# One inference step of a hybrid decoder layer: the transition from attention to experts reordered, and a front that accumulates the query projections over half of the features while the other half of the modulation arrives

## What is computed

```python
h = rmsnorm(x, ln_mix_g) * (1.0 + sc1) + sh1
z = h @ w_in                       # 19 column blocks of 512: queries are the first two
x = x + g1 * ((ga * oa + gb * ob + gc * oc) @ w_out)
h2 = rmsnorm(x, ln_ffn_g) * (1.0 + sc2) + sh2
logits = h2 @ router_w + router_b  # top 4 of 32 experts per token
...                                # per expert: w1 (1024 x 2048), gated, w2 (1024 x 1024)
x = x + g2 * f
```

## Time and profile before

| what | value |
|---|---|
| median of 3 runs | 1566.5 us (1562.74 to 1569.09) |
| the profiled execution's own time | 1566.85 us |
| its span in the trace | 1564.5 us |
| PE busy | 1479.6 us, 95% |
| mean granted PE clock | 0.973 of full speed |
| HBM read | 490.14 MB |

### The profile page before, as it was taken

The page is one execution under the profiler, slowest core; times in us unless marked ns, Lnnn a source line. Parts: engine busy times, 40 slices in busy tenths (PEclk is TensorE's granted clock), DMA queues, the critical chain, the costliest instruction groups (busy, mean ns, idle before and its releaser), DMA issues.

```text
span 1564.5 us, 21084 instructions
## 1 busy us (share of the span) xinstructions
PE 1479.6 (95%) x8234; PEld 628.3 (40%) x8235; DVE 648.6 (41%) x1001; ACT 338.3 (22%) x610; POOL 128.7 (8%) x118
## 2 busy tenths in 40 slices
PE   4989899999999978999999999999999999999997
PEld 3455455554555452333333333333333333333332
DVE  2141223445246472444353443443444435344444
ACT  2123332212223132212112121121121211212121
POOL 0000000213227703000000000000000000000000
PEclk8989999999999987999999999999999999999998
DMA  9663542342233975999999999999994999999994
GB/s 350 225 248 117 232 164 98 119 125 108 89 114 118 286 309 220 428 426 427 428 429 429 429 429 429 428 429 429 377 428 170 429 429 429 428 428 428 428 429 201
DMA packets 40269, 495.22 MB, mean 317 GB/s; under 512 B 5316, under 2 KB 5860, under 8 KB 11428
## 3 DMA queue, kind: packets, MB, share of 16 engines
q1 hardware_dynamic: 35700, 480.18, 74.2%
q0 software_dynamic: 4528, 14.46, 3.4%
HBM read 490.14 MB, written 4.47 MB: 316 GB/s over the span
## 4 chain that ended last, share of the span: by engine, by line
PE 81%; DMA 12%; DVE 3%; ACT 1%; POOL 1%; issue 1%; SPq 0%; POOLq 0%; DVEq 0%
PE ps L1866 25%; PE ps L1459 18%; PE ps L1891 14%; DMA memory<-in_w_moe 9%; PE ps L1470 4%; PE ps L1816 4%; PE ps L1801 4%; PE ps L1412 3%; DMA memory<-in_w_dense 1%; DMA memory<-mod_rows 1%; PE ps L1428 1%; PE ps L1873 1%; PE ps L1524 1%; DMA consts<-in_consts 1%; PE ps L1551 1%
## 5 line engine op out<-in xcount | busy, mean ns | idle before, releaser
L1866 PE MATMUL ps<-memory,arena 128*64 128x512 f32 x2176 | 483.9, 596 | 9.8 <-DMA memory<-in_w_moe 9.8
L1459 PE MATMUL ps<-memory,xT 128*128 128x512 f32 x672 | 308.5, 616 | 6.4 <-DMA memory<-in_w_dense 6.4
L1866 PEld LDWEIGHTS ps<-memory,arena 128*64 128x64 f32 x2176 | 152.3, 137 | 301.8 <-issue 277.0
L1891 PE MATMUL ps<-memory,arena 128*64 128x512 f32 x1088 | 248.4, 598 | 0.1
L1459 PEld LDWEIGHTS ps<-memory,xT 128*128 128x128 f32 x672 | 129.4, 197 | 163.4 <-issue 155.3
L1891 PEld LDWEIGHTS ps<-memory,arena 128*64 128x64 f32 x1088 | 72.3, 136 | 145.9 <-issue 134.7
L1388 DVE TENSOR_TENSOR R<-R,xT 128x1024 f32<-128x1024 f32 (+1 forms) x102 | 124.7, 1222 | 3.5
L1377 DVE TENSOR_SCALAR arena<-ps 128x512 f32<-128x512 f32 x34 | 23.5, 692 | 230.8 <-PE ps L1873 230.8
L1385 DVE SCALAR_TENSOR_TENSOR xT<-ps,arena,mod 128x1024 f32<-128x1024 f32 x68 | 87.1, 1281 | 10.1 <-PE ps L1816 10.1
L1816 PE MATMUL ps<-xT,arena 64*128 64x512 bf16 x630 | 87.6, 386 | 2.9 <-DVE xT L1394 2.9
L856 ACT ACTIVATE xT<-ps 128x512 f32<-128x512 f32 x35 | 20.9, 599 | 310.2 <-PE ps L1801 301.4
(11 more groups left out here) (299 smaller groups left out, 1189.6 us busy)
## 6 DMA issues: line engine op xcount, KB each, us to landing
memory<-in_w_moe SPq DMA_DIRECT2D x192, 2048.0 KB, 22.7
memory<-in_w_dense SPq DMA_DIRECT2D x33, 2048.0 KB, 8.6
memory<-in_state POOLq DMA_DIRECT2D x8, 256.0 KB, 7.3
out_sample_retention<-memory POOLq DMA_DIRECT2D x8, 256.0 KB, 5.2
memory<-mod_rows SPq DMA_DIRECT2D x4, 512.0 KB
arena<-in_b POOLq DMA_DIRECT2D x9, 128.0 KB, 2.6
R<-in_x_prompt SPq DMA_DIRECT2D x1, 1024.0 KB, 10.4
arena<-in_cache_kT POOLq DMA_DIRECT2D x8, 128.0 KB, 3.5
```

What stands on the lines that cost most here:

```text
L1459: last = mm(banks[t][0], xT[:, k, t * P:t * P + P], wv[:, k, :], start=(k == 0), stop=(k == KD - 1))
L1866: last = mm(ps[64 * a:64 * a + 64, half, :], xgT[:, k, j % 2, :], wv[:, k, HALF * a:HALF * a + HALF], start=(j % 2 == 0 and k == 0), stop= ...
L1891: last = mm(ps[64 * a:64 * a + 64, 2, :], actT[:, k, j - 4, :], wv[:, k, HALF * a:HALF * a + HALF], start=False, stop=(j == 5 and k == 3), ...
```

## The change

Three things change together.

**The front.** The order of the dense units becomes `ada` 2, 0, 3, 1, AKV, ...; AQ0 and AQ1 leave the ring and go to slots 3 and 4, and SP issues them right behind `ada` 0, without a wait. With scale and shift of features 0 to 511 there, PE accumulates k = 0 to 3 of four query pieces (AQ0 and AQ1, tiles 0 and 1) and of AQ0's tile 2, with `modulation(3)` and `modulation(1)` in between, and adds k = 4 to 7 later. The high four groups are copied out of PSUM unscaled first (`xT_raw`), since their banks are the ones that the pieces need, and scaled in place afterwards. The small matrix `ident` is the second transfer instead of the sixth. POOL's first loads wait for `ada1` instead of `ada0`.

**The transition's transfers.** The prompt's gain rows go to another place (`V[:, 1, :]`) and are loaded before the sample's first gate; expert unit 3 is issued behind the shift rows instead of ahead of them; DVE waits for the prompt's gain alone before the first residual.

**The transition's order.** On DVE `normalise(0)` stands behind `mean_square(1)`, `choose_experts(0)` and `(1)` follow one another, and `normalise(2)` stands behind `choose_experts(2)`. PE counts experts tile by tile with wider products, gathers the first block before the table's product, and POOL's `memset` of `y_parts` waits for `first_picked`.

```diff
-DENSE_ORDER = [("ada", 2), ("ada", 3), ("ada", 0), ("ada", 1), ("proj", AQ0), ("proj", AQ1), ("proj", AKV),
+DENSE_ORDER = [("ada", 2), ("ada", 0), ("ada", 3), ("ada", 1), ("proj", AKV),
...
+RING_UNITS = len(DENSE_ORDER)
+DENSE_ORDER += [("proj", AQ0), ("proj", AQ1)]
...
         sp.dma_start(silu_c, ins["c"]).then_inc(c_in, 16)
+        sp.dma_start(ident, ins["consts"][:, 0:P]).then_inc(select_in, 16)
         load_unit(0)
...
         load_unit(1)
+        load_unit(proj_unit(AQ0))
+        load_unit(proj_unit(AQ1))
         load_unit(2)
...
         load_rows(V[:, 0, :], 4, gate1_in)
+        load_rows(V[:, 1, :], 8, gain2_in)
         load_rows(V[0:64, 2, :], 4, gate1_in)
...
         sp.wait_ge(merged, 3)
-        load_rows(U[:, 2, :], 8, gain2_in)
-        load_rows(U[0:64, 1, :], 8, gain2_in)
-        load_expert_unit(3)
+        load_rows(U[0:64, 1, :], 8, gain2_sample_in)
         aux_filled(sp, "tm4")
...
         load_rows(T[0:64, 2, :], 6, shift2_in)
+        load_expert_unit(3)
         load_expert_unit(4)
...
+        for k in (4, 6):
+            X.tensor_copy(xT[:, k:k + 2, 0:SEQ], ps[:, k // 2, :].rearrange("p (k m) -> p k m", k=2)).then_inc(xT_raw, 1)
...
+        modulation(2)
+        turn_modulation(2)
+        modulation(0)
+        turn_first(low)
+        turn_modulation(0)
+        turn_first(high)
+        unit_arrived(pe, proj_unit(AQ0))
+        pe.wait_ge(xT_ready, 2)
+        for k in low:
+            if k >= 2:
+                pe.wait_ge(xT_ready, k + 1)
+            project_part(AQ0, 0, [k])
+        pe.wait_ge(xT_raw, 2)
+        project_part(AQ0, 1, low)
+        unit_arrived(pe, proj_unit(AQ1))
+        project_part(AQ1, 0, low)
+        modulation(3)
+        pe.wait_ge(xT_raw, 3)
+        project_part(AQ1, 1, low)
+        turn_modulation(3)
+        modulation(1)
+        pe.wait_ge(xT_modulated, 1)
+        project_part(AQ0, 2, low)
+        turn_modulation(1)
+        pe.wait_ge(xT_ready, 6)
+        pe.wait_ge(xT_modulated, 3)
+        for t in range(3):
+            if t == 2:
+                pe.wait_ge(xT_modulated, 4)
+            project_part(AQ0, t, high).then_inc(z_ready, 1)
+        for t in range(2):
+            project_part(AQ1, t, high).then_inc(z_ready, 1)
+        pe.wait_ge(z_used, Z_USED[AQ0, 2])
+        project_part(AQ1, 2, range(KD)).then_inc(z_ready, 1)
...
+        dve.wait_ge(gain2_in, 16)
+        fold_gain("p")
...
         mean_square(0)
-        inverse_root(0)
-        normalise(0)
...
         mean_square(1)
+        dve.wait_ge(gain2_sample_in, 16 * BATCH_S)
+        fold_gain("s")
+        normalise(0)
...
         choose_experts(0)
+        choose_experts(1)
         inverse_root(2)
+        choose_experts(2)
         normalise(2)
-        choose_experts(1)
-        choose_experts(2)
...
         aux_filled(pool, "lg2")
+        pool.wait_ge(first_picked, 1)
...
+        pe.wait_ge(routed, 1)
+        count_in(slice(0, 1), before, 0, True, True)
+        count_in(slice(1, 4), ones, 0, False, False)
         pe.wait_ge(routed, 2)
...
         gather_first()
+        pe.wait_ge(diag_ready, 1)
+        aux_free("table")
```

More of the change, by code:

```diff
@@ L951, in _ @@
+        X.tensor_copy(sample_T[:, high], turned_sample[:, high]).then_inc(xT_raw, 1)
+        for k in (4, 6):
+            X.tensor_copy(xT[:, k:k + 2, 0:SEQ], ps[:, k // 2, :].rearrange("p (k m) -> p k m", k=2)).then_inc(xT_raw, 1)
+        dve.wait_ge(sample_scaled, 1)
+        X.tensor_tensor(sample_of(sample_T, low), sample_of(sample_T, low),
+                        modT[:, 1, low, 1:].unsqueeze(3).to_broadcast(each), ALU.add).then_inc(xT_modulated, 1)
+        for n in (3, 1):
             copy_modulation(n)
@@ L1274, in _ @@
         residual(1, 0)
+        inverse_root(0)
         aux_filled(dve, "sl_rows")
@@ L1442, in _, with project_part @@
         z_pieces = iter(range(len(PIECES)))
+        def project_part(idx, t, ks):
+            wv = ring[:, dense_slot(proj_unit(idx)), :].rearrange("p (k c) -> p k c", k=KD)
+            banks = z_banks(idx)
+            for k in ks:
+                if t < 2:
+                    last = mm(banks[t][0], xT[:, k, t * P:t * P + P], wv[:, k, :], start=(k == 0), stop=(k == KD - 1), skip_group_check=True)
+                else:
+                    for a in range(2):
+                        last = mm(banks[2 + a][0], xT[:, k, 2 * P:TOKENS], wv[:, k, 256 * a:256 * a + 256],
+                                  start=(k == 0), stop=(k == KD - 1), skip_group_check=True)
+            return last
         def project(count):
@@ L1487, in _, with turn_first @@
             tr(aux_bank(f"mT{n}")[:, 0:P], mod[:, n, :], P).then_inc(aux_ready, 1)
-        project(9)
+        def turn_first(ks):
+            for t, r in enumerate(ROWS):
+                pe.wait_ge(normed, t + 1)
+                for k in ks:
+                    out = ps[:, 4, k * 64:k * 64 + 64] if t == 2 else ps[:, k // 2, k % 2 * SEQ + t * P:k % 2 * SEQ + t * P + P]
+                    last = tr(out, W[0:r, t, k * P:k * P + P], r)
+            last.then_inc(tr_ready, 1)
+        pe.wait_ge(silu_done, 1)
+        pe.wait_ge(select_in, 16)
+        low, high = range(4), range(4, KD)
+        modulation(2)
+        turn_modulation(2)
+        modulation(0)
+        turn_first(low)
+        turn_modulation(0)
+        turn_first(high)
[27 more added lines that the diff above has]
+        project_part(AQ1, 2, range(KD)).then_inc(z_ready, 1)
+        for _ in range(6):
+            next(z_pieces)
+        project(3)
         modulation(4)
@@ L1825, in filled @@
         def filled(j):
-            return DENSE_UNITS // DENSE_SLOTS if j < DENSE_SLOTS else 0
+            return sum(dense_slot(u) == j for u in range(DENSE_UNITS))
         def add_b2(i):
@@ L1835, in _ @@
         gather_first()
+        pe.wait_ge(diag_ready, 1)
+        aux_free("table")
+        mm(aux_bank("table")[:, 0:2 * MAX_BLOCKS], ones[0:MAX_BLOCKS, :], table_rows[0:MAX_BLOCKS].rearrange("p a g -> p (a g)"),
+           start=True, stop=True).then_inc(aux_ready, 1)
         for name in ("lg2", "pos", "table"):
```

138 lines of the change are left out of this document (62 added, 76 removed).

## The result

The changed kernel takes 1551.1 us (median of five runs, 1545.94 to 1553.56) against 1566.5: a ratio of 0.9904, 95% interval 0.9882 to 0.9927, 15.4 us less. The forecast was 1552.0, with 1546.5 to 1559.5 as its range. In the experiments, one run of `after_again` (6535.09 us) and one of `warm_filler` (3025.85) lie far outside all others and count in no median or ratio here.

A forecast was written before the change was run, and what follows sets the result against it. Weights, not PE, set the pace late in the expert loop, so the end hangs on when the expert units' stream starts. Front 5.5 plus transition 9.0 gave 14.5 us off 1566.85: 1552.35, forecast 1552, range 1546.5 to 1559.5.

The forecast's parts named there:

- The front, 5.5 us: Start to queries done: 7.5 us earlier by the new order, less 2.0 for low clock; ends 3.0 and 7.5.
- the 2.0 taken: Front, PE after its idle stretch: low clock costs 2.0 us, taken between nothing and 4.5.
- The lower end of that term: Front, low-clock cost: nothing, as the clock still read 1.00 until 30 us before.
- The transition, 9.0 us: Transition up to POOL's start: 9.7 us earlier, less 0.7 for POOL beside DVE; ends 7.5 and 10.
- (a): Transition: PE's 2.86 us wait for DVE, held by the shift rows, goes; 2.8 us gained.
- (b): Transition: DVE's choices in new order and PE's counting tile by tile end earlier; 3.2 us gained.
- (c): Transition: the gather starts 0.1 us behind the selection, at 581.08 instead of 584.84; 3.7 us gained.
- the 0.7: Transition: POOL's six subtractions, now beside DVE's table and gates, lose 0.7 us.
- PE had 4.95 us to spare: Before the loop's first gather: PE's slack covers `turn(1)` coming some 3 us behind the gather instead of 0.7.
- POOL was slowed: Rival, chance 0.13: POOL's splitting takes 17.8 us instead of 12.6, stream 5.2 us later, 1556.5 us.
- no unit of the front was waited for: Rival, chance 0.08, in the front: `ada` 1 comes at 47.5, 6.1 us past its need; 1558 us.
- the clock was up again by AQ0's first piece: Rival, chance 0.08, in the front: clock stays low through AQ0's first pieces; 1556.7 or 1560.1, 1558 in the middle.

The follow-up runs named there:

- after_again: The changed kernel run once more, unchanged, on the chip of the next three runs: 1550.7 us, ratio 0.9904 to the kernel before.
- warm_filler: Changed kernel plus 64 unused matmuls before `modulation(0)`, where PE stood idle: 1552.0 us, ratio 0.991 to the kernel before.
- front_only: Kernel before with the front of the change alone, transition and its transfers as before: 1558.0 us, ratio 0.995, 7.0 us less.
- vector_rest: Changed kernel with the sample tile's first subtraction on DVE and ACT's first two roundings before its take of turned tokens: 1551.3 us, ratio 0.9902.
- warm_and_rest: Changed kernel with 64 unused matmuls in PE's idle stretch, one subtraction moved to DVE and two ACT roundings earlier: 1551.1 us, ratio 0.9905.
- both_early: Changed kernel with DVE's gates before the table's wait, POOL's splits in tile order and unit 7 behind the second split: 1554.6 us, ratio 0.9937.

## Why the prediction was right

**The front, 5.5 us: measured 6.3 between the two traces.** The second unit came at 19.07, not 19.7. The low clock cost 1.26 us in the modulation (3.53 against 2.27) and 0.31 in the slices (1.49 + 1.43 against 2.61), 1.6 for the 2.0 taken; it was over by AQ0's first piece (10.54 for three half pieces, 3.5 each). PE's work from AQ0's start on, put at 40.9 us, took 41.3, with a gap of 1.53 for the 1.4. Mark 1 has 64.6 as its mean over the nine traces with the new front and no filler, and 69.83 and 72.52 over the two with the old one: 6.6 us, and `front_only` gave 7.0. The two old ones differ by 2.7 us themselves, half of it since the second modulation ran at half rate in the later one (3.64 us at 19.51, against 2.27). The lower end of that term, nothing because "the clock still read 1.00", rested on a reading that says nothing: the record of this trace said 1.00 too, at half rate. The Trainium skill, page TensorE: Matmul & The Clock Gate, Part 1, has the rule that an idle PE falls back to half rate; the two traces with a filler agree with it (1.95 us behind 2.79 idle, 3.42 behind 4.21).

**The transition, 9.0 us: measured 8.05 at unit 8.** Against 539.99 and 528.27, the start of the last long piece before and after, 11.7 us of offset, the steps are: (a) the row at 542.92 against 557.57, 2.9 for 2.8; (b) L1345 at 562.19 against 579.98, 3.1 for 3.2; (c) the gather at 563.34 against 584.84, 3.7 for 3.7. POOL's six took 12.85 us to SP's release against 12.57, 0.3 for the 0.7, all of it in the last subtraction (2.43 against 2.13). That makes 9.5 at unit 7. At unit 8 only 8.05 are left, 5.89 us behind unit 7 where it was 4.44 before (603.15 to 607.59), because unit 8 needs a unit that PE's late first block has used. The loop was 0.6 shorter, but it varies by 2.5 us over twelve traces. So the steps were right one by one, with one step missing that the forecast did not have. Their sum leaned on the one trace before: about 0.5 of (b), the cast beside POOL's `memset`, and 0.8 of (a) were not there in `front_only`, nor was 0.9 us of the gather, and measured from that trace the transition gave 5.8 us, below the range of 7.5 to 10 for the term.

**That step is the price of DVE beside POOL.** The forecast looked at what DVE does to POOL and found it small, rightly. It named what POOL does to DVE and put no price on it; "PE had 4.95 us to spare" was to cover all of it, and PE waited 7.69 us for its first expert block. The Trainium skill, page SBUF — State Buffer, section Who interferes with whom, says that whoever of the two comes second is blocked until the other's instruction has ended; a product of two SBUF operands, a copy and a cast were held here (6.59, 1.13 to 1.35, 2.07 us), and a reduction was not (0.80 to 0.83 beside POOL, 0.81 before). The trace goes further than the page: the product at L1383 went on through the ends of subtractions at 575.35 and 577.44 and ended at 579.93, 0.4 behind the end of a third at 579.51, so with POOL back to back the wait was far longer than one instruction. In `vector_rest` and `warm_and_rest` it took 2.43 us, held by one subtraction only; what decides between the two stays open.

**The bound.** "The end of the run hangs on when the stream of expert units starts" held: mark 3 to the end is 955.3 to 957.8 us in twelve traces, with PE's first expert block anywhere from 5.4 us (after, 582.41) to 15.0 us (both_early, 578.61) ahead of that mark. It broke only where PE stood for 13.41 us more. The bound is finer than the prediction had it: the mark is unit 8, and PE's first block sets that too when it is late, by 1.5 us here. The rivals did not come: POOL was slowed by 0.3 us only, no unit of the front was waited for, and the clock was up again by AQ0's first piece. One sum of the prediction is wrong: with all of the 39.5 us of PE's new front at double time the run would end near 1590 us, not 1577. It changes no term of the forecast.

**What was right by luck.** The profiled span fell 5.4 us more than the terms say, for the middle's sake. The table's middles spread over 8.5 us, so one trace against another cannot judge a change of this size; the terms were judged on marks around them. That the clock makes the difference is in the sums above; why one execution has more of these phases than another stays open, and with it whether the new front makes them rarer (17.1 and 18.8 us lost with the old front, 10.2 to 20.6 in eleven traces with the new). The forecast of 1552.0 for a measured 1551.1 is closer than its parts deserve: the front gave about 1 us more than its term, the transition 1 to 3 less.

## What to carry to other kernels

Look for the queue that the last bandwidth-bound stretch hangs on, and price a change by when that stream starts (here SP's issue of units 7 and 8), not by when the busiest engine does. When an operation is moved beside a run of GpSimd work, price both engines: here GpSimd lost 0.3 us and VectorE's 0.56 us product lost 6. Take such a price from more than one trace of the kernel before: the same old transition was 2.3 us shorter in a second one. Follow what is queued behind the one that is held, up to the next transfer.

## What the hardware showed that was not expected

- DVE's product of two SBUF operands, 128x384, took 6.59 us beside back-to-back POOL subtractions in three traces and 6.60 in a fourth, 2.43 in two more, and 0.56 where POOL was idle (six traces). In a gap of 1.62 us of POOL it ran at once.
- PEclk read 1.00 at 20 us of the changed kernel, where PE did 25 instructions of a kind of which it did 48 at 37 us. At the same place the records of four other traces read 0.50. Early in a trace the time of a known instruction tells the clock more surely than the record.
- Behind the same filler, 64 matmuls took 1.95 us after 2.79 us of idle time and 3.42 after 4.21, in one trace each.
- An untouched stretch of some 450 us varied by 8.5 us with the phases at the lower clock, over thirteen traces.
- Eight small row transfers issued by GpSimd behind unit 8 took 17 us to arrive; from SP's queue, ahead of unit 8, they took 9.7 and, in `both_early`, 4.7. The queue and the place in the stream are not told apart.
